# A gated DeltaNet layer inside a decoder trunk: the step table of its recurrence is rearranged

## What is computed

```python
qkv, z, b_raw, a_raw = split_cols(h @ w_in, ...)
qkv = silu(causal_depthwise_conv(qkv, conv_w)); q = l2norm(q) * 128 ** -0.5; k = l2norm(k)
beta = sigmoid(b_raw); g = -exp(a_log) * softplus(a_raw + dt_bias)
# per head and chunk, g summed up along the chunk:
decay = where(causal, exp(g_i - g_j), 0)
a_mat = where(strict, (k * beta) @ k.T * decay, 0)
t_inv = inverse(a_mat + eye)                 # unit lower triangular
u, w = t_inv @ (v * beta), t_inv @ (k * beta * exp(g))
intra = (q @ k.T) * decay
# over the chunks, in order:
v_new = u - w @ state
out = (q * exp(g)) @ state + intra @ v_new
state = state * exp(g_last) + (k * exp(g_last - g)).T @ v_new
o = rmsnorm(out, o_gain) * silu(z);  x = x + o @ w_out
```

## Time and profile before

| | |
|---|---|
| time, median of 3 runs | 2236.45 us (2236.19 to 2236.93) |
| profiled execution | 2235.43 us, its span 2233.6 us |
| PE busy | 2149.9 us, 96% of the span |
| DVE / ACT / POOL busy | 1051.4 / 787.2 / 278.7 us |
| TensorE clock granted, mean | 0.987 of full |
| the recurrent layer | about 1425 to 1800 us of the span |
| HBM traffic | 85 GB/s over the span |

### The profile page before, as it was taken

How to read it: one execution, slowest core, us unless ns; L and a number is a source line. 1 busy time by engine, 2 the same in 40 slices (tenths; PEclk the granted TensorE clock), 3 DMA queues, 4 the chain that set the end, 5 groups by cost and what they waited for, 6 DMA issues and landing times.

```text
span 2233.6 us, 25977 instructions
## 1 busy us (share of the span) xinstructions
PE 2149.9 (96%) x9662; PEld 1714.1 (77%) x9662; DVE 1051.4 (47%) x1573; ACT 787.2 (35%) x1143; POOL 278.7 (12%) x379
## 2 busy tenths in 40 slices
PE   7999999999999999999999999978888999999997
PEld 6888887656667888888788888766777787888886
DVE  4444444687644444432444432355555554444422
ACT  4333223224544333322333322444454443333221
POOL 1000000122111000000000000045445200000001
PEclk9999999999999999999999999989999999999999
DMA  4333322212113323332233332221111122333321
GB/s 169 94 94 96 120 92 70 76 49 66 47 57 94 94 94 98 111 98 79 89 99 94 98 116 87 67 64 53 51 56 48 58 87 93 95 102 94 113 91 51
DMA packets 55966, 190.18 MB, mean 85 GB/s; under 512 B 11728, under 2 KB 11728, under 8 KB 55888
## 3 DMA queue, kind: packets, MB, share of 16 engines
q1 hardware_dynamic: 53680, 189.00, 27.1%
q10 hardware_dynamic: 2208, 0.13, 0.1%
HBM read 186.74 MB, written 2.36 MB: 85 GB/s over the span
## 4 chain that ended last, share of the span: by engine, by line
PE 83%; POOL 6%; issue 5%; DVE 2%; ACT 2%; DMA 1%; SPq 1%; DVEq 0%; POOLq 0%; ACTq 0%
PE prod L436 26%; PE prod L438 25%; PE prod L437 25%; POOL rows L1509 2%; POOL rows_tmp L1506 2%; DMA blk<-blocks 1%; PE misc L638 1%; PE misc L569 1%; PE prod L526 1%; PE misc L587 1%; POOL b_lvl L1451 1%; DVE w_lo L1054 1%; ACT w_hi L779 1%; PE misc L549 0%; POOL t_inv L1515 0%
## 5 line engine op out<-in xcount | busy, mean ns | idle before, releaser
L436 PE MATMUL prod<-h_hi,w_hi 128*128 128x512 f32 x1856 | 764.5, 412 | 0.8 <-DVE w_lo L1054 0.4
L1054 DVE TENSOR_TENSOR w_lo<-raw,w_hi 128x1024 fp32r<-128x1024 f32 (+1 forms) x300 | 400.7, 1336 | 767.3 <-ACT w_hi L779 766.6
L438 PE MATMUL prod<-h_hi,w_lo 128*128 128x512 f32 x1856 | 728.4, 392 | 0.0
L437 PE MATMUL prod<-h_lo,w_hi 128*128 128x512 f32 x1856 | 727.9, 392 | 0.0
L779 ACT ACTIVATE w_hi<-raw 128x1024 fp32r<-128x1024 f32 (+1 forms) x317 | 356.2, 1124 | 606.6 <-PE prod L438 595.0
L436 PEld LDWEIGHTS prod<-h_hi,w_hi 128*128 128x128 f32 x1856 | 352.0, 190 | 101.4 <-issue 34.8
L438 PEld LDWEIGHTS prod<-h_hi,w_lo 128*128 128x128 f32 x1856 | 351.1, 189 | 75.1
L437 PEld LDWEIGHTS prod<-h_lo,w_hi 128*128 128x128 f32 x1856 | 352.3, 190 | 69.8 <-issue 7.3
L436 PE MATMUL prod<-a_hi,w_hi 128*128 128x512 f32 x704 | 278.1, 395 | 0.0
L438 PE MATMUL prod<-a_hi,w_lo 128*128 128x512 f32 x704 | 278.1, 395 | 0.0
L437 PE MATMUL prod<-a_lo,w_hi 128*128 128x512 f32 x704 | 278.1, 395 | 0.0
(11 more groups left out here) (229 smaller groups left out, 1848.8 us busy)
## 6 DMA issues: line engine op xcount, KB each, us to landing
raw<-in_w SPq DMA_DIRECT2D x253, 512.0 KB, 3.5
raw<-in_wd SPq DMA_DIRECT2D x64, 704.0 KB, 4.1
blk<-blocks SPq DMA_DIRECT2D x32, 128.0 KB
x<-in_x SPq DMA_DIRECT2D x8, 256.0 KB, 5.1
out<-y_out SPq DMA_DIRECT2D x8, 256.0 KB, 2.2
consts<-in_consts SPq DMA_DIRECT2D x1, 768.0 KB, 7.7
blocks<-a_mat SPq DMA_DIRECT2D x40, 4.0 KB, 1.4
raw<-in_w SPq DMA_DIRECT2D x2, 256.0 KB, 4.1
```

The source lines that it names most:

```text
L436: pe.matmul(bank, wh, hi, start=first and k == 0, stop=False)
L437: pe.matmul(bank, wh, lo, start=False, stop=False)
L438: ins = pe.matmul(bank, wl, hi, start=False, stop=last and k == tiles_n - 1)
L1054: dve.tensor_tensor(w_lo[:, n % 2, 0:w], raw[:, n % 4, 0:w], w_hi[:, n % 2, 0:w].bitcast(F32), ALU.subtract).then_inc(lo_ready, 1)
```

## The change

Only the recurrent layer's step table and what hangs on it change. (1) POOL's multiplication by the triangle leaves the step `mask` for a step of its own, `tri`, ten slots later; `rows` moves three slots up, so that POOL does `rows(g)` and `lvl7(g)` ahead of `tri(g + 1)`; `lvl7` moves up from 38 to 33. (2) `spread`, `decay` and `mask` move two and three slots down, behind `osum` of the head three before; the wait for that norm goes from `kk` to `decay` on PE, `osum` waits for one head fewer of `dif_ready`, and the load of the ln/exp table goes from `decay` to `osum` (for the first two heads to `rk`). (3) `turn` to `t7` and all of `CHAIN2` move three slots up. (4) `LATER` adds slots for head 0 (`kk`, `amat`, `blocks` 2, `gram` 1, `turn` to `t7` 4, `CHAIN2` 2) and head 1 (`turn` to `t7` 2). Slots of head g afterwards, relative to 24g: decay 4, mask 5, tri 12, kk 15, amat 17, blocks 18, rows 24, gram and lvl7 33, turn 36, y5 38, t7 48, new0 51, out 70, osquare 71, osum 74, fin 77. Slots of head 0 are then kk 17, amat 19, blocks 20, turn 40, and turn of head 1 is at 62, kk of head 1 at 39, kk of head 2 at 63.

```diff
@@ -112,12 +112,15 @@
-CHAIN1 = {"spread": -30, "decay": -27, "mask": -26, "kk": -13, "amat": -11, "blocks": -10, "lvl5": -9, "qdec": -6,
-          "lvl6": -5, "rows": -1, "rk": -1, "cv": 1, "gram": 5, "lvl7": 10, "turn": 11, "y5": 13, "t5": 15, "y6": 17,
-          "t6": 19, "y7": 21, "t7": 23}
-CHAIN2 = {"new0": 2, "st0": 4, "ks1": 6, "new1": 8, "st1": 10, "ks2": 12, "new2": 14, "st2": 16, "ks3": 18, "new3": 20,
-          "out": 21, "osquare": 22, "osum": 25, "fin": 28}
-SOONEST = {"spread": 10, "decay": 11, "mask": 12}
+CHAIN1 = {"spread": -28, "decay": -24, "mask": -23, "tri": -16, "kk": -13, "amat": -11, "blocks": -10, "lvl5": -9,
+          "qdec": -6, "lvl6": -5, "rows": -4, "rk": -1, "cv": 1, "gram": 5, "lvl7": 5, "turn": 8, "y5": 10, "t5": 12,
+          "y6": 14, "t6": 16, "y7": 18, "t7": 20}
+CHAIN2 = {"new0": -1, "st0": 1, "ks1": 3, "new1": 5, "st1": 7, "ks2": 9, "new2": 11, "st2": 13, "ks3": 15, "new3": 17,
+          "out": 18, "osquare": 19, "osum": 22, "fin": 25}
+SOONEST = {"spread": 10, "decay": 11, "mask": 12, "tri": 13}
+TURNED = ("turn", "y5", "t5", "y6", "t6", "y7", "t7")
+LATER = {0: {**{n: 4 for n in TURNED}, **{n: 2 for n in CHAIN2}, "kk": 2, "amat": 2, "blocks": 2, "gram": 1},
+         1: {n: 2 for n in TURNED}}
 TAP_SLOTS = (2, 3, 4)
 SILU_SLOT = {"k": 5, "q": 5, "v": 7}
 FIRST = 4
@@ -133,7 +136,7 @@
     for g in range(HEADS):
         for behind, chain in ((2, CHAIN2), (1, CHAIN1)):
             for name, at in chain.items():
-                slot = max(per * (g + behind) + FIRST + at, SOONEST.get(name, 0))
+                slot = max(per * (g + behind) + FIRST + at, SOONEST.get(name, 0)) + LATER.get(g, {}).get(name, 0)
                 out.setdefault(slot, []).append((g, name))
     for stages in out.values():
         stages.sort(key=lambda e: e[0])
@@ -654,6 +657,8 @@
                 if name == "decay":
                     if g >= 1:
                         pe.wait_ge(a_made, g)
+                    if g >= 3:
+                        pe.wait_ge(o_rstd, g - 2)
                     pe.wait_ge(gb_ready, g + 1)
                     for t in range(TT):
                         ins = pe.matmul(M[0][:, t, :], g_b[:, t, :], const["tri"], start=True, stop=True)
@@ -661,8 +666,6 @@
                 elif name == "kk":
                     pe.wait_ge(act_done, 3 * g + 1)
                     pe.wait_ge(dif_ready, g + 1)
-                    if g >= 3:
-                        pe.wait_ge(o_rstd, g - 2)
                     each(M[0], kf, kf).then_inc(kk_mm, 1)
                 elif name == "gram":
                     pe.wait_ge(act_done, 3 * g + 3)
@@ -728,7 +731,7 @@
                 elif name == "osum":
                     pe.wait_ge(o_sq, g + 1)
                     pe.wait_ge(a_made, min(g + 3, HEADS))
-                    pe.wait_ge(dif_ready, min(g + 4, HEADS))
+                    pe.wait_ge(dif_ready, min(g + 3, HEADS))
                     pe.matmul(misc[:, 0, :], const["ones"], sq_acc[:], start=True, stop=True).then_inc(o_sum, 1)
             for u in range(len(OD_UNITS)):
@@ -943,7 +946,8 @@
                         act.wait_ge(grow_mm, g)
                     act.activation(g_b[:], g_tok[:, :, g:g + 1].broadcast_to([P, TT, P]), ACT.Copy).then_inc(gb_ready, 1)
                 elif name == "decay":
-                    act.preload_act_table_set(LN_EXP)
+                    if g == 0:
+                        act.preload_act_table_set(LN_EXP)
                     act.wait_ge(grow_mm, g + 1)
                     if g == 0:
                         act.wait_ge(g_cum_in, 2)
@@ -971,7 +975,7 @@
                     for b in ACT_BLOCKS:
                         act.dma_start(blocks[g, b].rearrange("t k j -> k t j"), diagonal(b)).then_inc(blk_out, 16)
                 elif name == "rk":
-                    if g == HEADS - 1:
+                    if g < 2:
                         act.preload_act_table_set(LN_EXP)
                     act.wait_ge(rk2_ready, g + 1)
                     link(act.activation(rk[:], rk2[:], ACT.Ln))
@@ -1000,8 +1004,7 @@
                     act.wait_ge(out_mm, TT * (g + 1))
                     act.activation(sq[:, 1, :], prod[:, 1, :], ACT.Square).then_inc(o_squares, 1)
                 elif name == "osum":
-                    if g + 2 >= HEADS:
-                        act.preload_act_table_set(LN_EXP)
+                    act.preload_act_table_set(LN_EXP)
                     act.wait_ge(o_sum, g + 1)
                     link(act.activation(act_f[:, 1, :], misc[:, 0, :], ACT.Ln, bias=eps[:, 1:2], scale=1.0 / P))
                     act.activation(act_f[:, 1, :], act_f[:, 1, :], ACT.Exp, scale=-0.5).then_inc(o_rstd, 1)
@@ -1479,7 +1482,7 @@
                 add_squares(r)
             def stage_pool(g, name):
-                if name == "mask":
+                if name == "tri":
                     pool.wait_ge(dec_exp, g + 1)
                     pool.tensor_tensor(dec_t[:, g % 2], dec_t[:, g % 2], same(const["tri"]), ALU.mult).then_inc(dec_ready, 1)
                 elif name in ("lvl5", "lvl6", "lvl7"):
```

## The result

The changed kernel takes **2245.16 us** (median of 6, 2243.92 to 2250.71) against 2236.55 us (median of 6) in the same comparison: ratio 1.0043, 95% interval 1.003 to 1.0056, slower by 8.6 us. Forecast were 2248.2 us and slower. The profiled execution took 2244.59 us, its span 2242.8 us, 9.2 us more than before.

A forecast was written before the change was run, and what follows sets the result against it. Bound by the recurrent layer's per-head loop, closed by PE's program order: 41.9 us against 40.6. `t_inv(7)` 9.5 us later and 2.2 behind it make plus 11.7: 2248.2 us, itself 2243 to 2254, range with rivals 2237 to 2257.

The forecast's parts named there:

- The loop closed by PE's order: Recurrent layer: a head costs `kk`, `a_mat`, blocks, rows, `turn`, next `kk`, 40.6 us, as `kk(g+1)` stands behind `turn(g)`.
- Rows ahead of the mask, minus 3.0 to 3.5: POOL: `rows(g)` no longer behind the next head's `tri`, minus 3.0 us for head 4, minus 3.5 for head 2.
- rival 2: Faster: the three places cost nothing as `turn` no longer waits; 15 us of late rows gained, 2220 us; chance 0.06.
- The rows themselves, 13.3: POOL's rows with `t_inv`: 13.3 us instead of 14.1, minus 0.8, losing the cover of two taps of v.
- `turn` three places earlier, plus 4.9: PE: `kk(g+1)` three slots behind `turn(g)`, 5.5 us instead of 0.5 to 0.6; plus 4.9, bounds 4.0 and 6.3.
- The wait before `turn`: PE's wait for `t_inv`: 5 to 7 us a head, near 45 us in all.
- `kk` to `a_mat`, 5.5: DVE: `st2`'s state update ahead of `amat` where a `resid` stood; 5.5 us, plus 0.1, bounds 4.6 and 6.
- Blocks on ACT, plus 0.2: ACT sends `blocks(g)` behind copies of `y6(g-1)`; out takes 3.5 us instead of 3.3, plus 0.2, bounds 0 and 1.
- The way back, 14.0: Blocks' transfer back, called by SP: 14.0 us a head, taken from head 7 of the kernel before.
- The ends: First and last heads taken singly: `t_inv(7)` 9.5 us later in all, plus 2.2 us behind `turn(7)`.
- Next decay behind the norms, nothing: `osum` wait goes; PE may lose 2 us ahead of `turn` at decay and `gram`, covered by `turn`'s wait: nothing.
- Rival 1: Clock holds after `turn` if a stop over 2 us at `gram` splits PE's idle time; 2240 us, chance 0.17.

The follow-up runs named there:

- e2: Kernel before with only `kk` one slot up, ahead of `turn` on PE: 2222.58 us, ratio 0.9942.
- e7: e1 with `turn` to `t7` and the whole recurrence three slots up, decay, mask, `lvl7` and first heads' slots as before: 2263.75 us, ratio 1.013.
- e1: Kernel before with only POOL's `rows` two slots up, ahead of the next head's mask: 2221.76 us, ratio 0.9937.
- e4: Changed kernel with 16 extra matmuls on PE just ahead of `turn`'s wait, heads 3 to 7: 2241.4 us, ratio 1.0024 to the kernel before.
- e8: Changed kernel without its other places for the first heads (`LATER` empty): 2259.38 us, ratio 1.0104 to the kernel before.
- e9: Kernel before with `rows` and `lvl7` ahead of the next mask, `turn` to `t7` one slot down, `kk` left: 2212.45 us, ratio 0.9885.

## Why the prediction was right

- **The loop closed by PE's order.** Shown: e2 and e7 move nothing but the relation of `kk` and `turn` (e7 with the recurrence) and change the time by -13 us, and by +42 us against e1, of which 3.4 us lie behind the last `turn`.
- **Rows ahead of the mask, minus 3.0 to 3.5.** Right: 0.07 us from the blocks to the rows in every head; worth 14 us alone (e1), where rival 2 had priced it at 15.
- **The rows themselves, 13.3.** Right in the changed kernel: 13.3 to 13.6 us for heads 3 to 6, against 14.1. In e1, where they meet other work of DVE, they stayed at 13.9 to 15.0, so the gain probably hangs on what lies beside them. That it is the pair of ports shared by DVE and GpSimd, which the Trainium skill describes (page "SBUF — State Buffer", section "SBUF: two separate sides"), was not tried by itself; the first operation took 0.29 us here, and 0.74 in e2, where it starts beside a tap.
- **`turn` three places earlier, plus 4.9.** Right: 5.5, 5.5, 5.3 and 6.8 us behind `turn(3)` to `turn(6)`, for 5.5; and e4 divides it as taken. The wait before `turn` was smaller than forecast: 4.4 to 4.8 us for heads 3 to 6 where 5 to 7 were taken, and 37.1 us in all, not near 45. PE needed 31.2 us from `kk(4)` to that wait (1606.04 to 1637.26), not 29; 1.7 us at `gram` and 0.7 at `decay` are waits inside this stretch.
- **`kk` to `a_mat`, 5.5.** 5.43 in every head from 3 on, with the state update just ahead, as said.
- **Blocks on ACT, plus 0.2.** Nothing: ACT's issues started at 1612.12 us, 0.6 behind SP's, and SP's five take longer anyway (out 3.24 us for heads 3 and 4).
- **The way back, 14.0.** 13.2 to 13.6 us for heads 3 to 7. This term was too large by half a microsecond a head; the spacing came out at 41.3, not 41.9. It was the time of head 7 in the kernel before; heads 3 to 6 took 13.5 to 14.0 us there.
- **The ends.** `t_inv(7)` came 5.2 us late, not 9.5. Against the forecast, head by head: head 0 came 1.5 us sooner (its rows took 11.2 us where they had taken 13.3), head 1 0.5 and head 2 1.9 us (rows of 11.8 us instead of 13.3). Head 3 gave 1.3 back, since `t_inv(2)` was ready at 1557.36 us and PE came to `turn(2)` at 1559.92. Heads 4 to 6 made 1.6, in the main by the shorter way back, and head 7 nothing. Behind the last `turn` 4.0 us were added, not 2.2: the low clock lasted longer after the wait of 7.16 us (`turn` to `new2` 6.3 us instead of 5.3), and a new wait of 1.05 us for DVE stands at 1793.36 us. The misses partly cancel, which is luck: 9.2 us for 11.7.
- **Next decay behind the norms, nothing.** As said: the wait for the norm went, waits at `gram` of 1.7 us a head and at `decay` of 0.7 came, all covered by the wait at `turn`. Rival 1 had this split hold the clock. The split happened, but 4.44 us of idle were left at `turn(4)`, and the clock was 0.56 behind it. So the rival's outcome did not come. In e4 the clock held behind 2.91 us, but its premise, that a wait like the 2.27 us before `turn(6)` leaves the clock up, is not borne out: `turn(5)` of the kernel before waited as long, and the clock behind it was 0.66:

```profile
1684.90 0.66 PE L681 MATMUL misc<-consts,t_inv 128*128 128x128 f32 x4 [2.28 <-POOL t_inv L1515]
```

```profile
1684.90:1688.70 3.80, 3.80 (x19) 3.41 (x20) 1.59 (x12) 1.54 (x2) 1.17 (x1) 0.66 0.00 0
```

## What to carry to other kernels

When one engine's program is an interleaving by hand, look for a step that stands behind another only by order, and ask whether a long latency leads from it back to that other step: then each place between them is paid once a round. Moving up a step that waits gains nothing if what feeds its next round stands behind it; move the feeder ahead of the wait, even by one place (13 us here). And a gain that a rearrangement seems to give back is worth testing alone: the reordering on POOL was worth 14 us by itself.

## What was not expected of the hardware

A wait of PE cost more than its own length: behind the waits of 4.4 to 7.2 us at `turn` the next 3.8 us ran at a granted clock of 0.50 to 0.61, and in e7 and e8 at 0.50 to 0.62. For shorter waits the length did not settle it. Behind `turn` the clock was 1.00 after 2.27 us (before, head 6) and after 2.91 us (e4, head 4), but 0.66 after 2.28 us (before, head 5), and 0.56 after 1.98 us (e9, head 7; 1740.31 to 1744.11). What decides between them no run here shows. Sixteen useless matmuls, put where PE had to wait anyway, shortened the path behind the wait by 1.6 us, where they left 1.1 to 2.9 us of idle time.
